# A decoder layer with a mixture of 64 experts: weight matrices in halves, a fifth ring slot, smaller gather chunks, quads spread out, and a shorter routing

## The chip, the cores and the metric

The kernel runs on one core of a Trainium2 chip. The core has TensorE (matrix products), VectorE, ScalarE and GpSimd, a sequencer SyncE that here only issues transfers, and 16 DMA engines that move data from the chip's memory (HBM) into the core's buffer (SBUF). Matrix products are written into PSUM, which has eight banks. The metric is the device time of one execution in microseconds (us); less is better.

## The reference

One decoder layer for 256 tokens of width 1024, in float32. A mixer (stick-breaking attention, a recurrent block, cross-attention to a memory) is added to the input; then comes a mixture of experts, which is where nearly all of the time goes:

```python
h = x + mixer(rms_norm(x))
t = rms_norm(h)                                    # 256 x 1024
scores = sigmoid(t @ w_router)                     # 256 x 64
choice = scores + router_bias
grp_score = top_k(choice.reshape(256, 8, 8), 2).sum(-1)
emask = expert's group is among the best 4 of 8 groups
eidx  = top_k(where(emask, choice, -inf), 8)       # 8 experts per token
w     = scores[eidx] / (sum + 1e-20) * 2.5
routed = sum over the experts e of
         gate[:, e] * ((silu(t @ w_gate[e]) * (t @ w_up[e])) @ w_down[e])
out = h + routed + shared_expert(t)
```

The gate and up matrices of an expert are 1024 x 256 each, its down matrix is 256 x 1024; each takes 1 MiB, so an expert takes 3 MiB and the 64 experts take 192 MiB, each of which is read once.

## The kernel before

The program is written by hand for each engine: an engine runs its own list of instructions in order and waits on semaphores, which other engines and the DMA queue raise. SyncE's list is the queue of all weight transfers, so a wait in it holds back everything that stands behind it.

**Up to the experts.** The mixer takes the first 145 us. Then the second norm (`second_norm`, for the token tiles t = 0 and 1 of 128 tokens), the router's product on TensorE, and `route(t)` on VectorE, which picks 8 experts for every token with small instructions that each wait for the one before. In the meantime TensorE runs the shared expert's gate and up products (`shared_gate_up`), and then the counts of tokens per expert (L1537 to L1547), which wait for `route(1)`. From the counts VectorE makes `pick`, a matrix of ones and zeros that says which token stands in which slot (`build_pick`), and an order of the experts by number of tokens (`permute`, `ids`). The normed tokens `xn2` are split into two parts, `xhi` (ScalarE, L736) and `xlo` (GpSimd, L549), so that a gather by products with `pick` keeps full precision.

**Groups.** The experts are worked off in 26 groups of 128 token slots: a pair is two experts with 64 slots each, a quad is four experts with 32 slots each, and the wide pair is two experts in two groups (the weights are used twice). The order is: two pairs of fixed experts (`FIXED = 4`; the weights can be loaded before the routing is known), two quads, the wide pair, 15 pairs, five quads. `group(g)` on TensorE is, in order:

1. `gate_up` (L1580): for k = 0..7 the products of the gathered rows with the gate and up matrices, into bank U; it first waits for `gu_loaded` of all of its experts, and at the end raises `gu_ps`.
2. a part of the gather of the next chunk (L1554). A chunk is four groups (the first one two groups), and its eight steps k are shared out among the groups of the chunk before; ScalarE (L755) and VectorE (L1244) copy each result into `xg`.
3. transposes of the hidden rows and of the slot matrix, 0.56 us (L1586 to L1594).
4. `scatter` of the group before (L1610).
5. `down` (L1602), which waits for `d_loaded` and raises `y_ps` at its end.

**The ring.** `RING = 4` slots of 24 KB per partition hold one expert each: `ring_gu` (16 KB) and `ring_d` (8 KB). SyncE's loop takes the groups in order. For each it waits for `gu_ps` of the group that used the slot, expert by expert, and issues the gate and the up matrix (L363, L364), then waits for `y_ps` and issues the down matrix (L367):

```python
for e, r in zip(g.experts, chosen):
    sp.wait_ge(gu_ps, gu_end[gu_taken[e]] + 1)
    load_gate_up(sp, e, ranked(w_gate_e, r, KD), ranked(w_up_e, r, KD))
for e, r in zip(g.experts, chosen):
    sp.wait_ge(y_ps, 2 * d_end[d_taken[e]] + 2)
    load_down(sp, e, ranked(w_down_e, r, KH))
```

Before the first group the experts 1, 2 and 3, the shared expert's matrices and the fourth down matrix are in place; the gate and up matrices of the fourth expert follow when the first group's `gate_up` has ended.

## Time and profile before

| what | value |
|---|---|
| median of 3 runs | 683.92 us (682.54 to 684.01) |
| the profiled execution | 686.89 us, its span from first to last instruction 685.0 us |
| mean granted TensorE clock | 0.934 of full speed |
| TensorE busy | 578.9 us (85%) |
| VectorE, ScalarE, GpSimd busy | 206.0, 142.0 and 24.2 us |
| moved | 225.89 MB, mean 330 GB/s over the span |

A row of the chain of waits tells when a piece of the work that ended last began and how long it took; a window tells how busy each engine was in a stretch, what clock TensorE was granted, and how many GB/s the transfers moved. L with a number is a line of the kernel. TensorE has two clock levels, 2.4 GHz (1.00) and 1.2 GHz (0.50).

### The profile page before, as it was taken

To read this page: it belongs to the slowest core of one execution; us is meant where nothing else is said; L and a number is where in the kernel's file an instruction comes from. 1 tells how busy PE (TensorE), PEld (TensorE's weight loads), DVE (VectorE), ACT (ScalarE), POOL (GpSimd) and SP (SyncE) were. 2 spreads that over 40 slices of the span, in tenths; PEclk is the share of its full clock that TensorE was granted. 3 is DMA by queue.
4 is the path that set the end of the run, shared out by engine and by line. 5 is a ranking of instruction groups with operands and counts; after the bars stand their busy time and mean duration, and the time that the engine had idled before them with its cause. 6 is when DMAs were issued, how large, how long until landed. Compare 5 with 4: busy or idle time off the path is not lost.

```text
span 685.0 us, 7647 instructions
## 1 busy us (share of the span) xinstructions
PE 578.9 (85%) x2905; PEld 298.0 (44%) x2906; DVE 206.0 (30%) x497; ACT 142.0 (21%) x268; POOL 24.2 (4%) x75
## 2 busy tenths in 40 slices
PE   8999998998998596999999999999996817263545
PEld 6887774455553242544444454444443302021212
DVE  2328476777225011222231123123111201010103
ACT  5434237352111010211111111121111101010101
POOL 1001113020000000000000000000000000000000
PEclk9999999999999988999999999999998959695869
DMA  8954349610679999599999999999989797999892
GB/s 259 376 172 184 135 173 329 272 62 1 250 287 402 425 370 423 216 403 397 409 417 423 419 418 416 420 421 420 421 372 379 312 425 318 422 377 422 343 424 74
DMA packets 40830, 225.89 MB, mean 330 GB/s; under 512 B 4064, under 2 KB 11272, under 8 KB 15832
## 3 DMA queue, kind: packets, MB, share of 16 engines
q1 hardware_dynamic: 39688, 223.38, 80.6%
q0 software_dynamic: 528, 1.87, 1.0%
q8 instruction: 24, 0.39, 0.2%
q10 hardware_dynamic: 576, 0.13, 0.1%
q14 instruction: 14, 0.11, 0.0%
HBM read 224.32 MB, written 1.05 MB: 329 GB/s over the span
## 4 chain that ended last, share of the span: by engine, by line
PE 71%; DMA 18%; SPq 3%; DVE 3%; issue 3%; ACT 2%; DVEq 0%; ACTq 0%
PE ps L1580 29%; DMA ring_gu<-in_w_up_e 17%; PE ps L1602 10%; PE ps L1554 7%; PE ps L1340 6%; PE ps L1610 5%; PE ps L1456 4%; PE ps L1357 3%; SPq L363 1%; SPq L364 1%; PE ps L1503 1%; PE ps L1347 1%; DMA x_in<-in_x 1%; PE ps L1586 1%; PE ps L1592 1%
## 5 line engine op out<-in xcount | busy, mean ns | idle before, releaser
L1580 PE MATMUL ps<-ring_gu,xg 128*64 128x512 f32 (+1 forms) x992 | 184.7, 657 | 85.5 <-DMA ring_gu<-in_w_up_e 77.3
L1580 PEld LDWEIGHTS ps<-ring_gu,xg 128*64 128x64 f32 (+1 forms) x992 | 57.4, 135 | 209.4 <-issue 209.4
L1602 PE MATMUL ps<-ring_d,e_hT 128*64 128x512 f32 (+1 forms) x528 | 94.9, 597 | 0.2 <-DVE xg L1244 0.2
L1211 DVE TENSOR_TENSOR e_h<-e_sg,ps 128x256 f32<-128x256 f32 x26 | 16.2, 622 | 249.6 <-ACT e_sg L759 249.6
L1277 DVE SCALAR_TENSOR_TENSOR ylo<-ps,gslot,yhi 128x512 fp32r<-128x512 f32 x52 | 39.0, 751 | 116.7 <-ACT yhi L774 116.7
L759 ACT ACTIVATE e_sg<-ps 128x256 f32<-128x256 f32 x26 | 10.0, 383 | 271.4 <-PE ps L1580 271.4
L774 ACT ACTIVATE yhi<-ps,gslot 128x512 fp32r<-128x512 f32 x52 | 35.7, 687 | 116.7 <-PE ps L1602 116.7
L1602 PEld LDWEIGHTS ps<-ring_d,e_hT 128*64 128x64 f32 (+1 forms) x528 | 26.9, 125 | 54.2 <-issue 54.1
L1610 PE MATMUL ps<-yhi,S 128*128 128x512 f32 x104 | 43.1, 415 | 1.6 <-ACT yhi L774 1.6
L1610 PE MATMUL ps<-ylo,S 128*128 128x512 f32 x104 | 40.9, 393 | 0.0
L1554 PE MATMUL ps<-pick,xhi 128*128 128x512 f32 (+1 forms) x112 | 37.7, 418 | 0.0
L1554 PE MATMUL ps<-pick,xlo 128*128 128x512 f32 (+1 forms) x112 | 33.6, 382 | 0.0
L1456 PE MATMUL ps<-wo,yT 128*128 128x512 f32 x64 | 29.3, 601 | 0.0
L1554 PEld LDWEIGHTS ps<-pick,xhi 128*128 128x128 f32 x112 | 19.3, 193 | 21.3 <-issue 18.6
L1340 PE MATMUL ps<-hT,wA 128*128 128x256 f32 x128 | 27.8, 379 | 0.0
L1340 PEld LDWEIGHTS ps<-hT,wA 128*128 128x128 f32 x128 | 24.2, 190 | 3.3
L1244 DVE COPY xg<-ps 128x512 f32<-128x512 f32 x24 | 16.6, 691 | 24.3 <-PE ps L1554 24.3
L1554 PEld LDWEIGHTS ps<-pick,xlo 128*128 128x128 f32 x112 | 20.9, 193 | 4.3
L1610 PEld LDWEIGHTS ps<-yhi,S 128*128 128x128 f32 x104 | 19.6, 189 | 6.0 <-ACT yhi L774 2.5
L1610 PEld LDWEIGHTS ps<-ylo,S 128*128 128x128 f32 x104 | 19.6, 189 | 3.5
L755 ACT COPY xg<-ps 128x512 f32<-128x512 f32 x24 | 14.1, 587 | 17.5 <-PE ps L1554 17.5
L1456 PEld LDWEIGHTS ps<-wo,yT 128*128 128x128 f32 x64 | 11.5, 190 | 12.6 <-issue 11.8
(334 smaller groups left out, 545.8 us busy)
## 6 DMA issues: line engine op xcount, KB each, us to landing
ring_gu<-in_w_gate_e SPq DMA_DIRECT2D x64, 1024.0 KB, 10.2
ring_gu<-in_w_up_e SPq DMA_DIRECT2D x64, 1024.0 KB, 12.3
ring_d<-in_w_down_e SPq DMA_DIRECT2D x64, 1024.0 KB, 12.4
wA<-in_w_in SPq DMA_DIRECT2D x4, 1024.0 KB, 9.5
wo<-in_w_out SPq DMA_DIRECT2D x1, 4096.0 KB, 13.1
wR<-in_w_in SPq DMA_DIRECT2D x3, 1024.0 KB, 16.4
wV<-in_w_in SPq DMA_DIRECT2D x1, 2048.0 KB, 15.5
w_kv<-in_w_mem_kv SPq DMA_DIRECT2D x1, 2048.0 KB, 18.9
```

What stands on the lines that cost most here:

```text
L755: nc.scalar.copy(xg[(g.chunk + 1) % 2][:, k, :], ps[:, Y[0], :]).then_inc(xg_act, 1)
L774: nc.scalar.mul(yhi[:, half * 512:(half + 1) * 512], ps[:, Y[half], :], gslot[:, g.index % 2:g.index % 2 + 1]).then_inc(yhi_act, 1)
L1211: nc.vector.tensor_tensor(dst[:].rearrange("q k p -> q p k"), e_sg[:].rearrange("q (p k) -> q p k", k=KH), ps[:, U, DE:2 * DE].rearrange(" ...
L1244: nc.vector.tensor_copy(xg[(g.chunk + 1) % 2][:, k, :], ps[:, Y[1], :]).then_inc(xg_dve, 1)
L1277: nc.vector.scalar_tensor_tensor(ylo[:, c], ps[:, Y[half], :], gslot[:, g.index % 2:g.index % 2 + 1], yhi[:, c].bitcast(F32), ALU.mult, AL ...
L1340: last = mm(b[:, 0:SEQ], w[:, k, c:c + P], hT[:, k, :], start=k == 0, stop=k == KD - 1)
L1357: last = mm(b, a[:, k, c:c + P], w[:, k, :], start=k == 0 and m == 0, stop=k == KD - 1 and m == 2)
L1456: last = mm(ps[:, ACC[2 * t + half], :], yT[:, k, t * P:(t + 1) * P], wo[:, k, half * 512:(half + 1) * 512], start=k == chunks[0], stop=k ...
L1554: last = mm(ps[:, Y[k % 2], 0:n], part[:, t, k, :], pick[c % 2][:, t, 0:n], start=i == 0, stop=i == 3)
L1580: last = mm(ps[side * w:(side + 1) * w, U, :], rows(k, slice(side * w, (side + 1) * w)), ring_gu[n][:, :, k, :], start=k == 0, stop=k == K ...
L1602: last = mm(ps[side * w:(side + 1) * w, Y[half], :], e_hT[:, kk, side * w:(side + 1) * w], ring_d[n][:, kk, half * 512:(half + 1) * 512], ...
L1610: last = mm(ps[:, ACC[2 * t + half], :], to_token[:, t * P:(t + 1) * P], y[:, half * 512:(half + 1) * 512], start=first and i == 0, stop=f ...
```

## The change

- Gate and up matrices are loaded in halves of four k each (two transfers of 0.5 MiB in place of one of 1 MiB, 4 KB per partition and transfer in place of 8 KB), with a semaphore for each half; `gate_up` waits for the first half of all experts of its group, then for the second, and raises `gu_ps` after each, so that a half of a slot is released alone. SyncE's loop issues all first halves of a group, then all second halves, then the down matrices.
- `RING = 5`: the fifth slot lies where `wo` and the first chunk's buffers were. Chunks are two groups (13 chunks; `xg` has 8 KB per buffer, `pick` 2 KB), a gather step does two k with 256 columns each, and `xlo` overwrites `xn2`. `s_d` is loaded in two pieces, late, and used in group 3.
- `FIXED = 6`: three pairs of fixed experts. The gate and up matrices and the down matrix of the fourth are issued as soon as the output projection is done; the fifth down matrix comes early too.
- The quads are spread: after the wide pair come three pairs and a quad, again and again (14 pairs, 5 quads); the last group is a quad, as before.
- Routing: two small `tensor_scalar` and one product less per tile, the memset once and ahead, `picked` written directly by the comparison; `repl` is made once for both tiles while TensorE counts. `xlo` is computed on VectorE, for tile 0 ahead of the second norm of tile 1, for tile 1 between the two calls of `route`; GpSimd has nothing left there. ScalarE makes `xhi` of tile 0 earlier.

```diff
-    FIXED, HALF, TABLE = 4, 32, 8
+    FIXED, HALF, TABLE = 6, 30, 8
+    STEPS, SHARED = KD // 2, 3
-    RING = 4
+    RING = 5
...
-    plan = [("pair", None)] * 2 + [("quad", quads.pop(0)), ("quad", quads.pop(0)), ("wide", 0)]
-    plan += [("pair", r) for r in pairs] + [("quad", r) for r in quads]
+    plan = [("pair", None)] * (FIXED // 2) + [("quad", quads.pop(0)), ("quad", quads.pop(0)), ("wide", 0)]
+    while pairs or quads:
+        plan += [("pair", pairs.pop(0)) for _ in range(min(3, len(pairs)))]
+        plan += [("quad", quads.pop(0))]
...
-    chunks = [groups[0:2]] + [groups[i:i + 4] for i in range(2, NG, 4)]
+    chunks = [groups[i:i + 2] for i in range(0, NG, 2)]
...
-            g.index, g.chunk, g.column, g.step = groups.index(g), c, i * P, i * (KD // len(members))
-            g.steps = KD // len(members) if c + 1 < len(chunks) else 0
+            g.index, g.chunk, g.column = groups.index(g), c, i * P
+            g.steps = range(2 * i, 2 * i + 2) if c + 1 < len(chunks) else range(0)
...
+    gu_at = [o_ring + 24 * KB * s for s in range(4)] + [o_A + 16 * KB]
+    d_at = [o_ring + 24 * KB * s + 16 * KB for s in range(4)] + [o_R + 8 * KB]
...
+        K_HALF = [slice(0, KD // 2), slice(KD // 2, KD)]
+
+        def load_gate_up(sp, e, h, gate_src, up_src):
             n = gu_slot[e]
-            sp.dma_start(ring_gu[n][:, 0], gate_src).then_inc(gu_loaded[n], 16)
-            sp.dma_start(ring_gu[n][:, 1], up_src).then_inc(gu_loaded[n], 16)
+            sp.dma_start(ring_gu[n][:, 0, K_HALF[h]], gate_src[:, K_HALF[h]]).then_inc(gu_loaded[n][h], 16)
+            sp.dma_start(ring_gu[n][:, 1, K_HALF[h]], up_src[:, K_HALF[h]]).then_inc(gu_loaded[n][h], 16)
...
             sp.wait_ge(wo_ps, len(projections))
-            sp.dma_start(s_d[:], w_down_sh[0].rearrange("(p k) n -> p k n", k=KH)).then_inc(s_d_loaded, 16)
-
-            sp.wait_ge(gu_ps, 1)
-            load_gate_up(sp, 4, expert(w_gate_e, 3, KD), expert(w_up_e, 3, KD))
+            for h in range(2):
+                fixed_gate_up(4, h)
+            sp.wait_ge(ssq_act, 6)
+            fixed_down(4)
+            shared_down_src = w_down_sh[0].rearrange("(p k) n -> p k n", k=KH)
+            sp.wait_ge(route_dve, 2)
+            sp.dma_start(s_d[0][:], shared_down_src[:, 0]).then_inc(s_d_loaded, 16)
+
+            for h in range(2):
+                for e in (5, 6):
+                    sp.wait_ge(gu_ps, 2 * gu_end[gu_taken[e]] + h + 1)
+                    fixed_gate_up(e, h)
+            sp.wait_ge(s_hT_ps, NT)
+            sp.dma_start(s_d[1][:], shared_down_src[:, 1]).then_inc(s_d_loaded, 16)
+            sp.wait_ge(y_ps, 2 * d_end[d_taken[6]] + 2)
+            fixed_down(6)
...
-                    for e, r in zip(g.experts, chosen):
-                        if gu_taken[e] == 0:
-                            sp.wait_ge(s_gu_ps, NT)
-                        else:
-                            sp.wait_ge(gu_ps, gu_end[gu_taken[e]] + 1)
-                        load_gate_up(sp, e, ranked(w_gate_e, r, KD), ranked(w_up_e, r, KD))
+                    for h in range(2):
+                        for e, r in zip(g.experts, chosen):
+                            if gu_taken[e] == 0:
+                                sp.wait_ge(s_gu_ps, NT)
+                            else:
+                                sp.wait_ge(gu_ps, 2 * gu_end[gu_taken[e]] + h + 1)
+                            load_gate_up(sp, e, h, ranked(w_gate_e, r, KD), ranked(w_up_e, r, KD))
...
-            for t in range(NT):
-                pool.wait_ge(split_act, t + 1)
-                pool.tensor_tensor(xlo[:, t], xn2[:, t], xhi[:, t].bitcast(F32), ALU.subtract).then_inc(split_pool, 1)
...
-                link(nc.vector.memset(grp[:, t, 12:16], -HUGE))
...
-                link(nc.vector.tensor_scalar(grp[:, t, 0:GROUPS], grep[:, t, 0:GROUPS], -1.0, 1.0, ALU.mult, ALU.add))
-                link(nc.vector.tensor_scalar(grep[:, t, 0:GROUPS], grep[:, t, 0:GROUPS], -HUGE, None, ALU.mult))
...
-                link(nc.vector.tensor_tensor(cg, choice[:, t, :].rearrange("p (g e) -> p g e", g=GROUPS), taken, ALU.mult))
-                link(nc.vector.tensor_tensor(cg, cg, off, ALU.add))
+                link(nc.vector.scalar_tensor_tensor(
+                    cand[:, t, :].rearrange("p (g e) -> p g e", g=GROUPS),
+                    grep[:, t, 0:GROUPS].unsqueeze(2).to_broadcast([P, GROUPS, EG]), -HUGE,
+                    choice[:, t, :].rearrange("p (g e) -> p g e", g=GROUPS), ALU.mult, ALU.add))
...
-                link(nc.vector.tensor_scalar(repl[:, t, :], repl[:, t, :], HUGE, None, ALU.is_equal))
-                nc.vector.tensor_copy(picked[:, t, :], repl[:, t, :]).then_inc(route_dve, 1)
+                nc.vector.tensor_scalar(picked[:, t, :], repl[:, t, :], HUGE, None, ALU.is_equal).then_inc(route_dve, 1)
...
+            low_part(0)
             second_norm(1)
...
             route(0)
+            low_part(1)
             route(1)
...
-            def gather_step(c, k):
-                n = P * len(chunks[c])
-                for i, (part, t) in enumerate(((xhi, 0), (xhi, 1), (xlo, 0), (xlo, 1))):
-                    last = mm(ps[:, Y[k % 2], 0:n], part[:, t, k, :], pick[c % 2][:, t, 0:n], start=i == 0, stop=i == 3)
+            def gather_step(c, step):
+                for k in (2 * step, 2 * step + 1):
+                    o = ps[:, Y[step % 2], k % 2 * 2 * P:(k % 2 + 1) * 2 * P]
+                    for i, (part, t) in enumerate(((xhi, 0), (xhi, 1), (xlo, 0), (xlo, 1))):
+                        last = mm(o, part[:, t, k, :], pick[c % 2][:, t, :], start=i == 0, stop=i == 3)
...
+                    if k % 4 == 0:
+                        for n, count in entries:
+                            pe.wait_ge(gu_loaded[n][k // 4], count)
...
+                    if k % 4 == 3:
+                        last.then_inc(sem, 1)
```

## Rows read from the trace of the kernel before

**Rows 1.** The page: the span, and GB/s in 40 slices of 17.1 us.

```profile
span 685.0 us, 7647 instructions
...
GB/s 259 376 172 184 135 173 329 272 62 1 250 287 402 425 370 423 216 403 397 409 417 423 419 418 416 420 421 420 421 372 379 312 425 318 422 377 422 343 424 74
```

**Rows 2.** Windows: us, busy us (xinstructions) of each engine, TensorE clock, DMA share, GB/s.

```profile
264.00:507.00 243.00, 243.00 (x1126) 111.09 (x1124) 58.94 (x122) 42.89 (x80) 0.00 (x0) 0.99 0.97 402
507.00:669.00 162.00, 89.45 (x582) 32.98 (x578) 17.35 (x42) 12.79 (x24) 0.00 (x0) 0.78 0.92 375
```

**Rows 3.** The chain of waits in order of time: start us, us, what.

```profile
280.77 6.87 PE ps L1580 x32
287.64 2.06 PE ps L1554 x8
290.26 1.96 PE ps L1610 x8
292.21 3.58 PE ps L1602 x16
...
541.87 20.00 DMA ring_gu<-in_w_up_e
562.23 9.89 PE ps L1580 x64
...
672.42 3.62 PE ps L1602 x32
```

**Rows 4.** Windows: four stretches of the transfers; the last begins at an issue.

```profile
24.00:38.00 14.00, 14.00 (x66) 12.32 (x66) 6.91 (x8) 7.49 (x10) 0.00 (x0) 1.00 1.06 374
82.00:90.00 8.00, 8.00 (x38) 5.94 (x38) 3.61 (x10) 1.62 (x4) 1.07 (x4) 1.00 1.02 414
113.00:129.00 16.00, 14.69 (x61) 7.37 (x60) 12.81 (x31) 5.79 (x15) 0.72 (x1) 1.00 1.01 423
176.72:186.72 10.00, 9.78 (x40) 6.24 (x42) 3.64 (x9) 2.68 (x6) 0.00 (x0) 1.00 0.88 360
```

**Rows 5.** The timeline, SyncE's queue: start us, us, engine line.

```profile
176.72 0.33 SPq L363 DMA_DIRECT2D ring_gu<-in_w_gate_e  x1
...
538.20 0.34 SPq L363 DMA_DIRECT2D ring_gu<-in_w_gate_e  x1
```

**Rows 6.** The chain of waits from 160 us to the first group of experts.

```profile
163.72 4.02 PE ps L1554 x24
...
168.51 1.15 PE ps L1554 x8
169.66 7.02 PE ps L1580 x32
176.68 4.49 PE ps L1503 x10
```

**Rows 7.** The timeline, TensorE: the counts of the routing, and what it waited for.

```profile
160.22 0.20 PE L1537 MATMUL ps<-picked,upper 128*128 128x64 bf16 x1 [2.82 <-DVE picked L1095]
```

**Rows 8.** The timeline, VectorE, the routing of both token tiles.

```profile
150.02 1.78 DVE L1079 TENSOR_TENSOR grp<-top 128x8 f32<-128x8 f32 x1
...
152.44 1.94 DVE L1084 TENSOR_TENSOR grep<-grep,grp 128x8 f32<-128x8 f32 x1
...
156.27 0.22 DVE L1073 TENSOR_TENSOR choice<-score,rbias 128x64 f32<-128x64 f32 x1
...
158.22 0.17 DVE L1085 TENSOR_SCALAR grp<-grep 128x8 f32<-128x8 f32 x1
...
158.89 0.23 DVE L1091 TENSOR_TENSOR cand<-cand,grep 128x64 f32<-128x64 f32 x1
...
159.96 0.20 DVE L1095 CAST picked<-repl 128x64 bf16<-128x64 f32 x1
```

**Rows 9.** The timeline, GpSimd, beside the routing.

```profile
149.41 2.37 POOL L549 TENSOR_TENSOR xlo<-xn,xhi 128x1024 fp32r<-128x1024 f32 x1 [17.15 <-ACT xhi L736]
```

**Rows 10.** Groups of instructions, VectorE, shapes kept apart.

```profile
L959 DVE TENSOR_TENSOR ca_sq<-ca_raw 128x1024 f32<-128x1024 f32 x1 | 1.2, 1212 | 0.0
```

More of the change, by code:

```diff
@@ L728, in _ @@
                     evac_x2T(0)
+                    nc.scalar.copy(xhi[:, 0], xn2[:, 0]).then_inc(split_act, 1)
             def scores(t):
@@ L1109, in _ @@
             dve.wait_ge(consts, 3)
+            link(nc.vector.memset(grp[:, :, 12:16], -HUGE))
             def shared_evac(t):
@@ L1115, in _ @@
             route(0)
+            low_part(1)
             route(1)
+            dve.wait_ge(route_dve, 2)
+            link(nc.vector.tensor_scalar(repl[:], repl[:], HUGE, None, ALU.is_equal))
             dve.wait_ge(count_ps, 1)
@@ L1517, in shared_down @@
                     last = mm(ps[:, ACC[2 * t + half], :], s_hT[:, kk, t * P:(t + 1) * P],
-                              s_d[:, kk, half * 512:(half + 1) * 512], start=False, stop=False,
+                              s_d[kk][:, half * 512:(half + 1) * 512], start=False, stop=False,
                               skip_group_check=True)
@@ L1524, in _ @@
             router(0)
-            pe.wait_ge(gu_loaded[0], 32)
+            for h in range(2):
+                pe.wait_ge(gu_loaded[0][h], 32)
             pe.wait_ge(x1_dve, 12)
@@ L1620, in extra_pair @@
                 for k in range(KD):
-                    for t in range(NT):
-                        last = mm(ps[:, Y[k // 4], k % 4 * P:(k % 4 + 1) * P], xn2[:, t, k, :],
-                                  ov_pick[:, t, :].bitcast(F32), start=t == 0, stop=t == NT - 1)
+                    for j, (part, t) in enumerate(((xhi, 0), (xhi, 1), (xlo, 0), (xlo, 1))):
+                        last = mm(ps[:, Y[k // 4], k % 4 * P:(k % 4 + 1) * P], part[:, t, k, :], ov_pick[:, t, :],
+                                  start=j == 0, stop=j == 3)
                     if k % 4 == 3:
@@ L1672, in group @@
                     pe.wait_ge(caps_dve, 1)
-                gate_up(lambda k, c: wide_rows[:, k, c0 + c.start:c0 + c.stop], [gu_slot[e] for e in g.experts], gu_ps,
+                gate_up(lambda k, c: source[:, k, c0 + c.start:c0 + c.stop], [(gu_slot[e], 32 * gu_fill[e]) for e in g.experts], gu_ps,
                         chunk=g.chunk if g is chunks[g.chunk][0] else None)
```

177 lines of the change are left out of this document (83 added, 94 removed).

## The prediction

> **What bounds the kernel now.** I read the page first, for GB/s: from the thirteenth slice on most slices stand at 415 to 425, with dips, and the ninth and tenth stand at 62 and 1 [rows 1]. A kernel that moves 192 MiB of expert weights is then to be read by its transfers. The windows cut that part into two regimes. While pairs run, TensorE is busy for all of 243.0 us and the transfers run at 402; while the last quads run, TensorE is busy for 89.45 of 162 us at a mean clock of 0.78 and the transfers run at 375 [rows 2]. The chain of waits says why. A group costs TensorE 6.87 (`gate_up`) + 2.06 (gather) + 0.56 (transposes, 289.70 to 290.26) + 1.96 (scatter) + 3.58 (down) = 15.03 us [rows 3], for a pair as for a quad. A pair brings 6 MiB = 6.29 MB, which at 424 GB/s takes 14.84 us: TensorE leads by a hair. A quad brings 12 MiB, 29.7 us, so there the transfers lead, TensorE waits (the last `up` matrix lands 20.00 us after its issue) and then runs `gate_up` at the lower clock, 1.2 GHz, in 9.89 us where a full-speed one takes 6.87 [rows 3]. During a quad's `gate_up` all four slots are in use and nothing can be issued before it ends (L363 at 538.20 [rows 5]), so each quad also costs idle transfers. The reader is to see two parts, each held by the resource that the other leaves free: in total TensorE needs 26 x 15.03 = 391 us, the transfers of the experts need about 475 us, and the kernel spends 685.0 - 169.66 = 515 us from the first group to the end [rows 1, 6]. Whatever lets the queue run without pauses from an earlier moment is worth its full length.
>
> What the queue does when it is full: 423 GB/s with the 8 KB runs of the expert matrices, 414 in the window that lies inside the `wo` transfer, whose runs are 4 KB, 374 in the window of the input projection's matrices, whose runs are 1 and 2 KB. From an issue at 176.72 the next 10 us bring 360 instead of 424, so the start costs 10 x (1 - 360/424) = 1.5 us [rows 4].
>
> **When the first group starts.** TensorE's shared work before the counts ends at 160.22 - 2.82 = 157.40; it then waits 2.82 us for `picked` [rows 7]. Routing of tile 1 takes 156.27 to 160.16. Of it the two `tensor_scalar` (0.20 each from start to start), one product of two (0.26), the memset (0.10) and the cast (0.20) go: about 1.0 of 3.9, so 2.9 are left [rows 8]. In tile 0 two instructions on eight elements take 1.78 and 1.94 us, beside 0.17 for one as small; both end when GpSimd's `xlo`, 2.37 us from 149.41 and its twin after it, ends [rows 8, 9]. With that work gone from GpSimd they shrink by 3.4 us. VectorE pays for `xlo` itself: 1.21 us each by a product of the same 128x1024 [rows 10]; the first lies in its wait for ScalarE's square ahead of the second norm (0 to 0.1 us on the path), the second is on it. So: 149.2 + 2.9 + 1.2 + 2.9 = 156.2, ahead of 157.4. The wait goes, and 1.2 us are to spare; without that cover each further us of routing would cost one. GpSimd's queue holds nothing behind the removed work, and ScalarE makes `xhi` of tile 0 (one copy of 1024 columns) while it waits for the residual of tile 1. The new `repl` over both tiles lies beside the counts.
>
> Then TensorE no longer pauses. Before, after the pause, the gather's 24 products took 4.02 us where the last 8 took 1.15 [rows 6], so 32 take 4.6 at full speed against 5.2; shared products in between were slow too (160.86 to 163.72 for four of the ten that take 4.49 [rows 6], so 1.8 instead of 2.9). I take 2.8 + 0.6 + 1.1 = 4.5 us: group 0 starts at 165.2 instead of 169.66. Bounds: 2.8 if the clock falls anyway, nothing if routing is late.
>
> **TensorE per group.** The gather has 16 products of 256 columns for 8 of 512. At 1.15/8 = 0.144 each [rows 6] that is 2.30 for 2.06, so 15.27 a group. Bounds: 2.06, and 16 x 0.19 (a 128x128 weight load, if that set the pace) = 3.0. The copies out of the banks keep their number and size. `build_pick` comes twice as often with half the work, while `gate_up` runs; the extra waits inside `gate_up` cost nothing when the halves are there. SyncE issues 16 halves for a quad in place of 8 matrices; at 0.33 us of an issue [rows 5], or 0.5 with what stands around it, that is 8 us beside 29.7 us of transfers, hidden while the queue is full.
>
> **Bytes and rate.** Before the first group ends its first half there are now expert 1 to 4 and down 5 in place; the transfers of expert 4, after the output projection, fall into the slices of 62 and 1 GB/s [rows 1], which is cover enough. Left are 60 x 2 MiB in halves, 59 down matrices and half of `s_d`: 179.5 MiB = 188.2 MB, 125.8 of them in runs of 4 KB. For those I take 418 GB/s, between 414 and 423 and nearer to the row with the same runs, whose stretch also has the ends of one transfer in it: 301.0 + 62.4/0.424 = 147.2, together 448.2 us, 420 GB/s, 2.50 us a MiB. Bounds: 444 and 451.
>
> At one place a rule of the Trainium skill speaks against the change. DMA: Bandwidth & Descriptors says to batch transfers to at least 1 MiB (section Bandwidth) and gives a fixed 2.0 us for each beside bytes/436e3 us (section Anatomy of one DMA); were it paid for each half one after the other, 240 x 3.2 + 60 x 4.4 = 1030 us would come out, an estimate from that page. The rows disagree for queued transfers: 1 MiB each runs at 423 GB/s, 2.5 us [rows 4], not 4.4.
>
> **Pauses of the queue.** Bytes start at 165.2 + 3.4 (half of 6.87) + 1.5 = 170.1; before, the issue came at 176.72 [rows 5]. I follow SyncE's list against TensorE's clock.
> - Experts 5 and 6, 4 MiB, to 180.1. Behind them stands the wait for the shared transposes: group 0 has 6.9 + 4.5 + 2.3 + 0.6 + 0.4, so 179.9, bytes at 181.4: pause 1.3. The half of `s_d` ends at 182.6; down 6 waits for the end of group 0, 183.7, bytes at 185.2: pause 2.6.
> - Down 6 and the first halves of experts 7, 8, 9, 4 MiB, to 195.2. Expert 10, the fourth of the quad, needs the slot of a fixed expert of group 2, and all behind it waits. Group 1 ends at 183.7 + 15.3 + 0.8 = 199.8; group 2's first half at 203.2, bytes at 204.7: pause 9.5.
> - From then on 48 MiB are free to go before the next such spot (expert 26, fourth of the first spread quad): to 324.6. TensorE: group 2 to 215.1; group 3 with the shared down (7.1) and 2.3 of waits to 239.7; group 4 waits 5.9 for its second halves and pays 2.7 for the clock, 263.5; two to 280.8; then 15.3 each, group 9 starts at 326.7, its first half ends at 330.1, bytes at 331.6: pause 7.0.
> - Then three pairs and a quad bring 30 MiB, 74.9 us, against 4 x 15.3 + 2.7 on TensorE: the slots come free before the queue gets to them, and there is no pause. 123 MiB x 2.50 = 307.1, to 638.7.
>
> Sum: 170.1 + 448.2 + 20.4 = 638.7. The last down matrices arrive while TensorE is past `gate_up`; `down` to the end took 685.0 - 672.42 = 12.6 us [rows 1, 3], and data is usable up to 2.8 us after my count of bytes (538.20 + 1.5 + 19.8 against 562.23 [rows 3, 5]; I take 1.8). 638.7 + 1.8 + 12.6 = 653.1 for the span, against 685.0. The profiled execution's span is 1.1 above the median of the runs, so 652.0. Followed in the same way, the kernel before pauses for 5.5 us near 193 and for 8.3 us near 281; its slices 12 and 17 lack 17.1 x (1 - 287/424) = 5.5 and 17.1 x (1 - 216/424) = 8.4 us [rows 1], which is my ground for trusting the pauses.
>
> **Rivals.**
> *Halves run slower.* This is the case on the other side: shorter runs and twice as many transfers. (It is the mechanism of the Trainium skill's page DMA: Bandwidth & Descriptors, section Bandwidth.) If 4 KB halves went at the 374 GB/s of the shortest runs [rows 4], 336.4 in place of 301.0 us: 652 + 35 = 687. It decides at 125.8/(301.0 + 31.9) = 378 GB/s. Against it: 414 with the same runs. 4%.
> *The queue in order starves at every quad.* Pauses of 7 us at the four later quads too, less what TensorE catches up: 652 + 14 = 666, at worst 680. For it: one blocked fourth expert holds all behind it. Against: 75 us of transfers for 64 us of products. 17%.
> *The queue hardly pauses.* No pause at 324.6 and 423 for all: 652 - 7 - 4 = 641. It needs TensorE earlier at group 9 by 7 us, for which I see little. 10%.
> *TensorE is dearer* (16 x 0.19 a group): 0.7 more in each of the eight groups up to the second large pause, 652 + 6 = 658, within my range; later it hides.
> *No effect:* only if the quads' waits come back elsewhere in full, 2%.
>
> **Numbers.** My own case, 646 to 660, 67%. With the case below and most of the starving one the range is 642 to 668. A difference under 0.2% is about what a measurement of this kernel can't tell from none: faster 0.93, same 0.02, slower 0.05.
>
> **What will show it.** Windows of 350 to 600 at 418 to 422 GB/s with no idle; group 0 at 165.2 and no wait of the counts for `picked`; the two slow instructions at 0.2 us; a pause near 195 to 205 and one near 325 to 332; TensorE's waits for gate and up spread over the quads in pieces of 2 to 6 us, not 15. I am wrong if the full queue stands under 410 in the halves, or if windows between 350 and 600 show idle transfers while SyncE waits for `gu_ps`.

## The result, and the profile after

The changed kernel takes 669.53 us in the median of four runs (668.13 to 670.6), beside 683.96 us (682.54 to 686.55) of the kernel before on the same chip: a ratio of 0.9775 with the interval 0.9753 to 0.9797. It is faster, as forecast, but by 14.4 us where 31.9 were forecast, and 1.5 us outside the range of 642 to 668. The miss in the median is 17.5 us (669.53 against 652.0). It has two parts. The span of the profiled execution is 667.3 us where the sum had 653.1, so 14.2 us are of the kernel. The other 3.3 us come from the last step, from span to median: the forecast took off 1.1, because the one profiled execution before had a span 1.1 above the median; after the change the profiled span lies 2.2 below the median. That is the scatter of single executions, not a matter of the kernel, and without it the median would lie inside the range.

The page of the changed kernel, to be laid beside [rows 1]; GB/s is in 40 slices of 16.7 us:

```profile
span 667.3 us, 8385 instructions
...
GB/s 256 375 196 189 80 236 274 342 68 155 283 253 278 418 411 411 413 412 414 267 328 414 409 413 411 417 411 412 412 408 415 414 412 412 394 413 413 411 398 93
DMA packets 59699, 225.95 MB, mean 339 GB/s; under 512 B 6160, under 2 KB 13368, under 8 KB 51464
```

Two things are to be seen. From the twenty-second slice on there is not one dip as deep as those that [rows 1] show to the end: the queue stays full. But the level is 408 to 417 in all of them but three (394, and 398 and 93 at the end), where [rows 1] has 416 to 425 wherever nothing stops it. And the slices 20 and 21 (317 to 350 us) stand at 267 and 328. The windows say it in figures (columns as in [rows 2]):

```profile
165.00:200.00 35.00, 34.96 (x176) 16.80 (x174) 9.92 (x29) 6.46 (x13) 0.00 (x0) 1.00 0.74 255
165.00:345.00 180.00, 166.58 (x914) 78.55 (x914) 45.44 (x125) 27.87 (x53) 0.00 (x0) 0.98 0.90 348
...
198.00:204.00 6.00, 6.00 (x30) 2.01 (x28) 4.48 (x16) 0.82 (x2) 0.00 (x0) 1.00 0.06 23
204.00:208.00 4.00, 2.88 (x18) 1.42 (x15) 3.08 (x16) 0.39 (x1) 0.00 (x0) 1.00 0.92 236
328.00:335.00 7.00, 7.00 (x36) 2.35 (x34) 1.50 (x2) 1.30 (x2) 0.00 (x0) 1.00 0.09 32
340.00:345.00 5.00, 5.00 (x25) 1.73 (x27) 0.75 (x1) 1.02 (x2) 0.00 (x0) 1.00 1.00 271
400.00:600.00 200.00, 169.37 (x934) 77.43 (x932) 39.40 (x93) 27.60 (x51) 0.00 (x0) 0.91 1.02 411
...
645.00:650.00 5.00, 5.00 (x32) 1.25 (x24) 0.00 (x0) 0.00 (x0) 0.00 (x0) 0.56 0.94 392
650.00:655.00 5.00, 3.77 (x30) 2.28 (x26) 1.64 (x6) 0.76 (x2) 0.00 (x0) 1.00 0.31 129
```

The chain of waits gives the times of the steps (it answers to [rows 3, 6]); the line numbers of `gate_up`, gather, scatter and `down` are now L1607, L1578, L1638 and L1630:

```profile
159.87 2.87 PE ps L1578 x24
...
164.65 7.02 PE ps L1607 x32
...
206.00 0.91 DVE pick L1154 x4
207.04 2.14 PE ps L1578 x16
...
275.42 2.11 PE ps L1578 x16
...
329.54 3.46 PE ps L1607 x16
...
628.43 15.96 DMA ring_gu<-in_w_up_e
...
644.53 6.09 PE ps L1607 x32
...
652.55 1.97 PE ps L1638 x8
654.52 3.67 PE ps L1630 x32
```

TensorE does not pause before the first group (the 24 gather products behind the counts take 2.87 us where [rows 6] have 4.02), and group 0 starts at 164.65. The two slow instructions of [rows 8] now stand at 0.17 us, in the timeline of VectorE:

```profile
150.26 0.17 DVE L1100 TENSOR_TENSOR grp<-top 128x8 f32<-128x8 f32 x1
...
150.95 0.17 DVE L1104 TENSOR_TENSOR grep<-grep,grp 128x8 f32<-128x8 f32 x1
```

SyncE's queue in the timeline, the last issue ahead of each of the two long waits and the first behind it:

```profile
189.19 0.56 SPq L367 DMA_DIRECT2D ring_gu<-in_w_up_e  x1
202.66 0.33 SPq L366 DMA_DIRECT2D ring_gu<-in_w_gate_e  x1
...
319.56 0.35 SPq L367 DMA_DIRECT2D ring_gu<-in_w_up_e  x1
333.49 0.34 SPq L366 DMA_DIRECT2D ring_gu<-in_w_gate_e  x1
```

And the waits of TensorE (total us, times, longest):

```profile
PE ps L1607 <- DMA ring_gu<-in_w_up_e: 57.1, 21, 6.3
```

**Where the 14.2 us went.** By the forecast 154.5 us of transfers at 420 GB/s, 64.9 MB, would have been moved by 345 us (from 170.1, less 20.4 of pauses). The window 165 to 345 has 180 x 348 = 62.6 MB. The 2.3 MB that are missing cost 5.5 us at 411 GB/s; of these 3.4 are the rate (154.5 x 420/411 = 157.9) and 2.1 are longer pauses and dips. After 345 us 123.3 MB were left in the forecast: 293.6 us at 420, 300.0 at 411, 6.4 more. By this count the last byte is due at 650.6, and the span ends 16.7 later instead of 14.4: 2.3 more. Two things meet there. The transfers thin out (129 GB/s from 650 to 655). And by the chain TensorE's own way is as long: the last `up` matrix lands at 644.39, the second half of the last `gate_up` takes, after 4.45 us without work, 6.09 us (granted clock 0.56 from 645 to 650) where a half at full speed takes 3.46 (329.54 above), and `down` starts at 654.52 right behind the scatter, with no wait for a transfer in between. Together 3.4 + 2.1 + 6.4 + 2.3 = 14.2. The rate alone is 9.8 of it.

That is an account of where the difference lies, not yet its cause. Two questions went to the chip: what halves do to the rate, and whether the two large pauses, which the forecast held for a given, were the ring's or the list's.

### The profile page after: what moved, and what is told of

It is laid out like the page before. It is cut to its first block, busy times and chain, and to the rows that moved or that the text cites. A ratio compares the mean times of both kernels' runs of the same rounds, so it can differ in the third digit from the quotient of the medians.

```text
span 667.3 us, 8385 instructions
## 1 busy us (share of the span) xinstructions
PE 590.5 (88%) x3097; PEld 311.1 (47%) x3098; DVE 204.8 (31%) x513; ACT 141.5 (21%) x264; POOL 20.5 (3%) x81
## 4 chain that ended last, share of the span: by engine, by line
PE 60%; DMA 25%; SPq 8%; ACT 3%; DVE 2%; issue 2%; DVEq 0%; ACTq 0%
DMA ring_gu<-in_w_up_e 24%; PE ps L1607 20%; PE ps L1630 8%; PE ps L1362 6%; PE ps L1578 5%; SPq L367 4%; PE ps L1638 4%; SPq L366 4%; PE ps L1478 4%; PE ps L1379 3%; PE ps L1525 2%; PE ps L1369 1%; DMA x_in<-in_x 1%; PE ps L1335 1%; PE ps L1440 1%
## 5 line engine op out<-in xcount | busy, mean ns | idle before, releaser
L1607 PE MATMUL ps<-ring_gu,xg 128*64 128x512 f32 (+1 forms) x1056 | 210.7, 693 | 57.1 <-DMA ring_gu<-in_w_up_e 57.1
L1607 PEld LDWEIGHTS ps<-ring_gu,xg 128*64 128x64 f32 (+1 forms) x1056 | 65.1, 140 | 198.8 <-issue 198.6
L1630 PE MATMUL ps<-ring_d,e_hT 128*64 128x512 f32 (+1 forms) x528 | 94.9, 597 | 3.0 <-issue 3.0
L1630 PEld LDWEIGHTS ps<-ring_d,e_hT 128*64 128x64 f32 (+1 forms) x528 | 27.4, 125 | 56.6 <-issue 56.6
L1578 PE MATMUL ps<-pick,xhi 128*128 128x256 f32 x208 | 45.0, 298 | 1.1 <-DVE pick L1154 1.1
L1638 PE MATMUL ps<-yhi,S 128*128 128x512 f32 x104 | 43.2, 415 | 1.6 <-ACT yhi L795 1.6
L1578 PEld LDWEIGHTS ps<-pick,xhi 128*128 128x128 f32 x208 | 32.1, 190 | 21.3 <-issue 21.2
L1578 PE MATMUL ps<-pick,xlo 128*128 128x256 f32 x208 | 41.8, 282 | 0.0
L1638 PE MATMUL ps<-ylo,S 128*128 128x512 f32 x104 | 40.9, 393 | 0.0
L1578 PEld LDWEIGHTS ps<-pick,xlo 128*128 128x128 f32 x208 | 32.2, 191 | 0.0
L1638 PEld LDWEIGHTS ps<-yhi,S 128*128 128x128 f32 x104 | 19.6, 189 | 5.9 <-ACT yhi L795 2.5
L1638 PEld LDWEIGHTS ps<-ylo,S 128*128 128x128 f32 x104 | 19.6, 189 | 3.5
## 6 DMA issues: line engine op xcount, KB each, us to landing
ring_d<-in_w_down_e SPq DMA_DIRECT2D x64, 1024.0 KB, 17.1
```

The source lines that it names most:

```text
L1578: last = mm(o, part[:, t, k, :], pick[c % 2][:, t, :], start=i == 0, stop=i == 3)
L1607: last = mm(ps[side * w:(side + 1) * w, U, :], rows(k, slice(side * w, (side + 1) * w)), ring_gu[n][:, :, k, :], start=k == 0, stop=k == K ...
L1630: last = mm(ps[side * w:(side + 1) * w, Y[half], :], e_hT[:, kk, side * w:(side + 1) * w], ring_d[n][:, kk, half * 512:(half + 1) * 512], ...
L1638: last = mm(ps[:, ACC[2 * t + half], :], to_token[:, t * P:(t + 1) * P], y[:, half * 512:(half + 1) * 512], start=first and i == 0, stop=f ...
```

## The experiments

Ratios are to the kernel before, with their intervals. "Whole" means that each gate and up matrix is one transfer of 1 MiB. All cuts of code are excerpts; "..." marks what is left out.

### The queue by itself

Five kernels only transfer the experts' matrices, through a ring of five slots, with no products; each was executed once. `s_whole_8k` has whole matrices in runs of 8 KB; `s_half_4k` the halves in the order of the change; `s_whole_4k` whole matrices cut into the same runs of 4 KB; `s_half_8k` halves by partitions; `s_first_halves` all first halves and then all second ones, without the down matrices.

```
# s_whole_8k
sp.dma_start(ring_gu[s][:, 0], rows(w_gate_e, e, KD))
# s_whole_4k
sp.dma_start(ring_gu[s][:, :, H[0]], rows(w_gate_e, e, KD).rearrange("p (h k) n -> p h k n", h=2))
# s_half_4k, s_first_halves
sp.dma_start(ring_gu[s][:, 0, H[h]], rows(w_gate_e, e, KD)[:, H[h]])
# s_half_8k, Q[h] = 64 partitions
sp.dma_start(ring_gu[s][Q[h], 0], rows(w_gate_e, e, KD)[Q[h]])
```

> Only the transfers of the 64 experts (192 MiB, 201.3 MB), in whole matrices of 1 MiB with 8 KB runs, one after the other through five slots; no products, the output is zeros. Both theories expect the 423 GB/s of the queue before the change: 476 us of transfers, 480 to 488 us in all.

> The same bytes, but gate and up in halves of 0.5 MiB with 4 KB runs, in the order of the changed kernel (pairs: first halves, second halves, downs); no products, zeros out. Theory H (the halves themselves fill the queue less well): 412 GB/s as in the changed kernel's windows of 400 to 500 us, so 488 us of transfers, 12 us more than the whole matrices. Rival K (the lower rate comes from what runs beside the transfers in the kernel): no difference, within 1 us of the whole matrices.

> Whole matrices of 1 MiB, but laid down so that each run is 4 KB; as many transfers as with 8 KB runs. If the run's length is the price (H1), it costs the same 12 us as the halves; if the number of transfers and their semaphore writes is the price (H2), it costs nothing.

> Halves of 0.5 MiB with 8 KB runs (64 partitions each), as many transfers as in the changed kernel. H1 (run length): as fast as whole matrices with 8 KB. H2 (number of transfers): 12 us slower, like the halves with 4 KB runs.

> Only transfers, no products, zeros out: the first halves of gate and up of all 64 experts, then all second halves, without down matrices (128 MiB, 134.2 MB). Theory D (a queue that holds only halves of one kind, each leaving out every other 4 KB of the memory, moves less, as after the pauses of the changed kernel, 217 to 303 GB/s): 240 to 300 GB/s throughout, 450 to 560 us. Rival (the low rate belongs to the first microseconds after an idle queue): 413 GB/s, 325 us and some 10 around it.

The spans are 486.2, 498.5, 495.6, 832.9 and 338.4 us. Of the 12.3 us between the first two, 9.4 come with the run length alone (`s_whole_4k`) and 2.9 between that and the halves, which differ from it in the number and in the order of the transfers. `s_half_8k` says nothing on the number: with half of the partitions in a transfer it took 1.7 times as long, which neither H1 nor H2 foresaw. Windows of three of them, in the middle and at the start (columns: us, VectorE, GpSimd, clock, DMA share, GB/s); first `s_whole_8k`:

```profile
20.00:300.00 280.00, 0.00 (x0) 0.00 (x0) 1.00 1.01 422
```

then `s_whole_4k`:

```profile
20.00:300.00 280.00, 0.00 (x0) 0.00 (x0) 1.00 1.02 414
...
3.00:4.00 1.00, 0.00 (x0) 0.00 (x0) 1.00 0.97 385
4.00:5.00 1.00, 0.00 (x0) 0.00 (x0) 1.00 1.05 426
```

and `s_half_4k`:

```profile
20.00:300.00 280.00, 0.00 (x0) 0.00 (x0) 1.00 1.02 413
...
3.00:4.00 1.00, 0.00 (x0) 0.00 (x0) 1.00 0.99 266
4.00:5.00 1.00, 0.00 (x0) 0.00 (x0) 1.00 0.87 201
5.00:6.00 1.00, 0.00 (x0) 0.00 (x0) 1.00 0.81 233
6.00:8.00 2.00, 0.00 (x0) 0.00 (x0) 1.00 1.02 412
```

The full queue makes no difference between 1 MiB and 0.5 MiB: 414 and 413. It is the run that counts, 4 KB or 8 KB. The low start of the halves is not the lot of first halves as such: `s_first_halves` has 262, 242, 205 and 225 GB/s from 2 to 6 us, and then 409 from 20 to 300, with nothing but first halves. That refutes theory D and bears out its rival. So in a stream of nothing but halves the gate and up matrices go at 409, where the forecast took 418. Two parts of 409 and one of 422 (the down matrices keep runs of 8 KB) give 413, which is what both mixed streams show.

### The parts of the change

`whole` is the changed kernel with whole matrices, released when `gate_up` has ended:

```diff
-            sp.dma_start(ring_gu[n][:, 0, K_HALF[h]], gate_src[:, K_HALF[h]]).then_inc(gu_loaded[n][h], 16)
-            sp.dma_start(ring_gu[n][:, 1, K_HALF[h]], up_src[:, K_HALF[h]]).then_inc(gu_loaded[n][h], 16)
+            sp.dma_start(ring_gu[n][:, 0], gate_src).then_inc(gu_loaded[n][0], 16)
+            sp.dma_start(ring_gu[n][:, 1], up_src).then_inc(gu_loaded[n][0], 16)
...
-                    for h in range(2):
+                    for h in (1,):
...
-                    if k % 4 == 0:
+                    if k == 0:
```

> The changed kernel with gate and up matrices loaded whole (1 MiB, 8 KB runs) and released when gate_up ends; all else as changed. Theory H (halves cost rate, 412 against 420 GB/s, and release in halves brings about 3 us by the prediction's own count of the queue): the full queue back at 420, about 9 us less for rate and 3 to 4 us more for pauses, so 662 to 665 us. Rival K (rate is not of the halves): 412 stays and the early release is missed, 672 to 676 us.

656.43 us, 0.9569 (0.9542 to 0.9596): 13 us faster than with halves. Loading in halves, which the forecast had as the part that shortens the pauses, is the part that takes half of the gain back. Theory H was right on the rate, but with 662 to 665 it took the release in halves for a small gain and left out the order of the halves, which is taken apart further down. Windows of `whole`:

```profile
165.00:345.00 180.00, 168.22 (x928) 79.77 (x930) 46.84 (x131) 28.43 (x54) 0.00 (x0) 0.97 0.90 364
...
400.00:600.00 200.00, 168.16 (x952) 78.65 (x949) 39.14 (x93) 27.56 (x51) 0.00 (x0) 0.92 1.01 421
```

421 beside 411 in the same stretch, and 364 beside 348 up to 345 us, although a whole matrix needs the end of `gate_up`, not its middle.

`spread_only` adds the spread quads to the kernel before; `unspread` and `whole_unspread` take them out of the changed kernel and of `whole`:

```diff
-    while pairs or quads:
-        plan += [("pair", pairs.pop(0)) for _ in range(min(3, len(pairs)))]
-        plan += [("quad", quads.pop(0))]
+    plan += [("pair", r) for r in pairs] + [("quad", r) for r in quads]
```

> The kernel before with the quads spread (three pairs, a quad) and nothing else. Theory: the quads' waits for transfers (some 15 us each for the last four) are paid for by the transfers that run ahead in the pairs; with four slots and whole release a quad still stops the queue once. Expected 665 to 672. Rival (four slots can't hold a quad and its successor, so each quad stalls as before): 680 to 686.

> The changed kernel with the quads at the end as before. Theory (spreading is the largest part): the pairs are set by TensorE at 15.1 us while the transfers have nothing to make up, and the quads at the end by the transfers; only the pauses between quads are shorter by the halves: 676 to 682. Rival (fifth slot and halves do most): 667 to 672.

> Whole matrices, five slots, six fixed experts, the quads at the end. If spreading pays only when the transfers can run at full rate (the count of the queue gives 2 us for it), 657 to 660; if spreading costs something, as the pair 669.5 (spread) and 667.2 (at the end) with halves suggests, 653 to 656.

1.001 (0.9991 to 1.0028), 0.9745 (0.9723 to 0.9767) and 0.9574 (0.9555 to 0.9592, beside 0.9569 of `whole`): the spreading is worth nothing, with four slots or with five. The expectations that gave it a price (665 to 672 for `spread_only`, 676 to 682 for `unspread`) missed. It is a balance of two effects. Without the spreading TensorE waits longer at the end and less in the middle, and the pause at the first late quad is not gone but comes later (337 and 331 GB/s in the slices 30 and 31 of `unspread`). So `whole_unspread` moves more up to 345 us (376 GB/s from 165 to 345 beside 364 of `whole`) and less after it (414 from 345 to 500 us and 415 from 500 to 625, beside 421). With halves it is the same: 369 beside 348, then 402 and 400 beside 412 and 411. Spreading together with the order of `adjacent_release`, below, was not taken apart.

`route_only` gives the kernel before the short routing and `xlo` on VectorE, with `x1_sq` moved to free room:

```diff
-            for t in range(NT):
-                pool.wait_ge(split_act, t + 1)
-                pool.tensor_tensor(xlo[:, t], xn2[:, t], xhi[:, t].bitcast(F32), ALU.subtract).then_inc(split_pool, 1)
...
+            low_part(0)
...
+            low_part(1)
```

> The kernel before with the shorter routing and xlo on VectorE only (the square's scratch moved by 4 KB so that it doesn't meet xlo). The first group starts 4.5 to 5 us earlier; the rest follows, so 679 to 680. Rival (the start is early, but the transfers set the rest and take it back): 683 to 684.

680.76 us, 0.9944 (0.9922 to 0.9966): 3.8 us less, near the 679 to 680 expected. Its group 0 starts at 165.18 us, 4.5 before the 169.66 of [rows 6].

`whole_ring4` is `whole` with four slots. `FIXED = 6` and the rest stay; the fixed experts that have no slot at the start, the fourth among them, follow as slots come free; beside the line shown, only these loads are put in another order:

```diff
-    RING = 5
+    RING = 4
```

> Whole matrices and all else of the changed kernel (six fixed experts, chunks of two groups, spread quads, short routing), but four slots; the fourth expert's gate and up wait again for the first group. The count of the queue gives 31 us more than with five slots: 680 to 688. Rival (the early start of the routing and the small chunks carry the gain, the slot only its own 3 MiB, 7.4 us): 662 to 666.

684.04 us, 0.9973 (0.9956 to 0.9989), as the theory had it. With all other parts in place the fifth slot, and the earlier loads that it allows, is worth 27.6 of the 29 us of `whole`. The parts do not add up: the routing alone brings 0.56% in `route_only`, and all parts but the slot together 0.27%. The slot alone, in the kernel before, was not run; its room comes from the smaller chunks. Windows of `whole_ring4`, late:

```profile
345.00:500.00 155.00, 133.41 (x742) 62.67 (x739) 31.36 (x73) 22.15 (x41) 0.00 (x0) 0.93 0.96 396
500.00:625.00 125.00, 97.25 (x544) 44.10 (x545) 22.65 (x55) 15.94 (x29) 0.00 (x0) 0.88 0.96 396
```

and of `whole`:

```profile
345.00:500.00 155.00, 131.73 (x752) 61.36 (x748) 32.16 (x75) 21.84 (x41) 0.00 (x0) 0.92 1.01 421
500.00:625.00 125.00, 106.43 (x597) 49.81 (x586) 25.45 (x60) 18.43 (x34) 0.00 (x0) 0.94 1.01 421
```

With four slots a quad holds all of them, and the queue dips once a quad: of the slices after 376 us in the page of `whole_ring4` three stand at 330 to 341 GB/s, 70 to 85 us apart as the quads are, and the others at 415 to 424 up to the last one. With five it does not, 396 against 421.

### What in the halves costs 13 us

`whole_4k` is `whole` with the runs of 4 KB; like `whole` it waits for the whole matrices before `gate_up`, while the versions in halves wait for half by half. `half_major` is the changed kernel, halves in its own order, but each half waits for the end of the whole `gate_up`. `half_adjacent` is `half_major` with both halves of an expert one behind the other. `adjacent_release` is the changed kernel with nothing else than that order.

```diff
# half_major
-                                sp.wait_ge(gu_ps, 2 * gu_end[gu_taken[e]] + h + 1)
+                                sp.wait_ge(gu_ps, 2 * gu_end[gu_taken[e]] + 2)
# adjacent_release, the only edit
-                    for h in range(2):
-                        for e, r in zip(g.experts, chosen):
+                    for e, r in zip(g.experts, chosen):
+                        for h in range(2):
```

> The version with whole matrices (656.4 us; transfers of 1 MiB, released at the end of gate_up), laid down so that every run is 4 KB: first half of gate, first half of up, second half of gate, second half of up. Theory: the run length is three quarters of the lower rate (9.4 of 12.3 us with transfers alone, of which some 300/475 fall into the full stretch that sets the end), so 662 to 664. Rival (the 13 us between halves and whole matrices are pauses and dips at restarts): 656 to 658.

> The changed kernel, halves in its own order (all first halves of a group, then all second halves), but a slot is released only when gate_up has ended. Theory O (the order is what costs: behind the blocked first half of a quad's fourth expert stand three second halves, 3 MiB, 7.5 us, that whole matrices have behind them already at the pause): still there, so 669 to 673. Rival N (the number of transfers and dips cost it): the same 669 to 673; this run is the base for the next.

> As half_major, but first and second half of each expert are issued one behind the other. Theory O: the 3 MiB go ahead of the pause, 7 to 9 us less than half_major, 661 to 664, near the whole matrices in 4 KB runs (660.9). Rival N (256 more transfers and their dips): no change against half_major.

> The changed kernel with only the order turned: first and second half of an expert one behind the other, each half released alone as in the change. Theory O: 660 to 663, and what release in halves is worth is its distance to half_adjacent (the count gives 1 to 3 us). Rival N: 669 to 670, as changed.

| kernel | order of the halves | released | us | ratio | GB/s 165:345 | 400:600 |
|---|---|---|---|---|---|---|
| `half_major` | by half | whole | 677.42 | 0.9893 (0.9868 to 0.9919) | 337 | 410 |
| the change | by half | by half | 669.53 | 0.9775 (0.9753 to 0.9797) | 348 | 411 |
| `whole_4k` | none, 4 KB runs | whole | 660.93 | 0.9642 (0.9627 to 0.9658) | 368 | 413 |
| `half_adjacent` | by expert | whole | 658.53 | 0.9629 (0.9602 to 0.9656) | 370 | 413 |
| `whole` | none, 8 KB runs | whole | 656.43 | 0.9569 (0.9542 to 0.9596) | 364 | 421 |
| `adjacent_release` | by expert | by half | 654.11 | 0.9554 (0.9527 to 0.9580) | 379 | 413 |

Each cause can be read between two rows. The order alone: 0.9775 to 0.9554, 15 us, and 0.9893 to 0.9629, 18 us. The runs: `whole` to `whole_4k`, 5 us. The number of transfers (128 more): `whole_4k` to `half_adjacent`, no difference clear of noise, and 413 GB/s in both late windows. This pair also differs in when `gate_up` may start, so it shows only that the two together are worth nothing. The release by halves: `half_adjacent` to `adjacent_release`, 5 us, and 8 us in the other order, more than the expectations gave it (1 to 3): so `half_major` is slower than the 669 to 673 expected, and `half_adjacent` (661 to 664) and `adjacent_release` (660 to 663) are faster. Theory O holds in its direction, rival N falls. SyncE's queue in `adjacent_release` shows how the order does it:

```profile
192.81 0.40 SPq L367 DMA_DIRECT2D ring_gu<-in_w_up_e  x1
202.56 0.33 SPq L366 DMA_DIRECT2D ring_gu<-in_w_gate_e  x1
...
318.95 0.43 SPq L367 DMA_DIRECT2D ring_gu<-in_w_up_e  x1
327.84 0.33 SPq L366 DMA_DIRECT2D ring_gu<-in_w_gate_e  x1
```

and its chain of waits has group 9 at:

```profile
324.23 6.87 PE ps L1607 x32
```

It waits from 193.2 for the same thing as the change from 189.8, the slot of the quad's fourth expert. But twelve transfers have gone out since 186.50 instead of six since 186.60: the second halves of experts 7, 8 and 9, whose room was free in both kernels, no longer stand behind the blocked first half of expert 10. Those are 3 MiB, 7.6 us of transfers, during which the queue is not idle. At the next quad it is the same, and there the pause goes: by then TensorE has waited less for matrices and starts group 9 at 324.23 instead of 329.54, so the queue's wait ends at 327.84 instead of 333.49. Windows of `adjacent_release`:

```profile
165.00:200.00 35.00, 34.95 (x176) 16.76 (x174) 9.93 (x28) 6.36 (x13) 0.00 (x0) 1.00 0.82 291
165.00:345.00 180.00, 171.31 (x966) 80.12 (x966) 46.78 (x127) 28.12 (x53) 0.00 (x0) 0.98 0.98 379
320.00:345.00 25.00, 25.00 (x153) 10.46 (x155) 5.56 (x11) 4.09 (x7) 0.00 (x0) 1.00 1.02 406
```

406 GB/s from 320 to 345 us, where the change has its pause. By 345 us 68.2 MB are moved, 5.6 more than in the change; at 413 GB/s that is 13.6 us, of the 14.8 by which the span is shorter (652.5). What is left lies in the rate, 413 for 411.

The Trainium skill says in DMA: Bandwidth & Descriptors, section Bandwidth, to batch transfers to at least 1 MiB. Its measurements there, and those behind the fixed 2.0 us that the forecast cites, are of transfers issued from GpSimd; here SyncE issues them. For queued transfers of this kernel the runs do not bear that out: `half_adjacent`, with 256 transfers of 0.5 MiB, takes what `whole_4k` takes with 128 of 1 MiB in the same runs (0.9629 and 0.9642).

### Smaller suspects

`whole_last` loads only the last quad in halves, so that TensorE may start its last `gate_up` earlier. `hoist` reads the numbers of the next group's experts ahead of the waits (SyncE spends 3.05 us on four such reads before 186.60, while expert 7 could go). `pick_first` is `whole_last` with `list_extra`, 24 small instructions on VectorE, each behind the one before, moved behind the picks of the second chunk.

```diff
# pick_first
+                if g.index == 2:
+                    dve.wait_ge(caps_dve, 1)
+                    list_extra()
...
-                if g.index == 1:
-                    dve.wait_ge(caps_dve, 1)
-                    list_extra()
# hoist
+            chosen = choose(order[0])
...
+                    if at + 1 < len(order):
+                        chosen = choose(order[at + 1])
```

> The changed kernel with whole matrices (the version of 656.4 us), but the last quad's gate and up in halves. In the trace of the whole version the last quad's gate_up starts when all of its 8 MiB have landed and ends after the last down matrix; in the changed kernel the second half alone is left. Theory: 4 to 5 us shorter than whole, 651 to 653. Rival (the last down matrices set the end either way): 655 to 657.

> The changed kernel with SyncE's reads of the next group's expert numbers placed before its waits (3 us between the issues at 183.2 and 186.6 are such reads). Theory V (they delay the transfers and all that follows): 3 us less than the changed kernel, 666 to 667. Rival (the following pause is ended by TensorE's group 2, not by the queue, so nothing moves): 669 to 670.

> Whole matrices with the last quad in halves (654.4 us), and list_extra, 5.4 us of small VectorE work, behind the picks for group 3 in place of ahead of them. It takes away 1.1 us for which group 2's gather waited for its picks. If TensorE's way to the pause at 330 us sets the end, 653 to 654; if it is taken up by the quads' waits for transfers, no change, 654 to 655.

`whole_last` is at 0.9568 (0.9545 to 0.9592), no difference to `whole`, where 4 to 5 us were expected. `hoist` is at 0.9778 (0.976 to 0.9795), none to the change: the first issue comes at 184.03 instead of 186.60, but the wait still ends at 202.56. `pick_first` is at 0.9524 (0.9505 to 0.9542), 653.26 us, the lowest median: 3 us better by the ratio than `whole_last`, 1.2 us by the medians (654.44). In the changed kernel the gather of group 2 waits for its picks, because VectorE works through the list first:

```profile
200.49 0.21 DVE L1204 TENSOR_TENSOR cnt<-cnt,caps 128x64 f32<-128x64 f32 x1
...
205.82 0.15 DVE L1229 CAST n_extra<-end 128x1 int32<-128x1 f32 x1
206.00 0.90 DVE L1154 TENSOR_TENSOR pick<-iota,posv 128x128 fp32r<-128x128 f32 x4
```

In `pick_first` they change places, and the gather follows `gate_up` (200.76 + 6.87 = 207.63) with no wait:

```profile
202.20 0.89 DVE L1165 TENSOR_TENSOR pick<-iota,posv 128x128 fp32r<-128x128 f32 x4
203.00 0.22 DVE L1215 TENSOR_TENSOR cnt<-cnt,caps 128x64 f32<-128x64 f32 x1
```

That the wait is gone is shown; that it is what makes `pick_first` faster is not. The wait is 1.1 us long, and in the profiled executions TensorE reaches group 9 at 329.12 in `pick_first` and at 328.04 in `whole_last`, later and not earlier. The order of `adjacent_release` together with the picks of `pick_first` was not tried; it would show whether the two gains add up.

## Why the prediction was right and where it was wrong

**When the first group starts: right.** 165.2 was forecast, 164.65 came, with no wait for `picked`. The four shared products ahead of the gather take 1.91 us (1.8 in the forecast); the gather's 32 take 2.87 + 1.14 = 4.0 where 4.6 stood, which is most of the 0.5 us.

**TensorE per group: right in kind, 0.2 us too high.** The 16 gather products take 2.11 us, not 2.30.

**Bytes and rate: the step that failed, a mis-sized term.** For the 125.8 MB of halves I took 418 GB/s, between 414 and 423, although the row with the same runs had 414 [rows 4]. A stream of halves alone runs at 409, the mix with down matrices at 413, the changed kernel at 411. So 188.2 MB take 458 us instead of 448.2, and my upper bound of 451 did not hold them either, for the lower value that I allowed, 414, lies above the 409 that such a stream reaches. The term is 9.8 us short; with it put right and nothing else the forecast would have been 662, and 7.7 us off instead of 17.5. Of the 9.8 us some 7.5 are the length of the runs (188.2 MB at 413 GB/s take 455.7). The other 2.3 are 411 against 413: the kernels with the order by half stand at 410 and 411, those with the order by expert at 413; why is open.

**Pauses of the queue: right in place, in size together with the dips, wrong in cause.** Two pauses near 195 to 205 and 325 to 332 were forecast; issues resume at 202.66 and 333.49. The first, 9.5 us in the forecast, is some 6 us of idle queue (198 to 204 at 23 GB/s), for the transfers ahead of it ran slower than counted, and a dip follows it (236 GB/s from 204 to 208). The bytes moved by 200 us come out even: 35 x 255 = 8.9 MB, and 8.5 MiB in the forecast. The second, 7.0 in the forecast, is 6.5 us long by its window (328 to 335 at 32 GB/s), but some 3 us late, because group 9 starts at 329.54 rather than 326.7; 1.1 of that is the wait for the picks, which the forecast had at nothing. (The working's "two to 280.8" reads as two groups; its times only come out with one group of 15.3 and 2 us of waits, and group 6 starts at 283.62.) Of the 2.1 us that were missing by 345, most is the dip behind it, which I had not foreseen: 5 x (1 - 271/411) = 1.7. What was wrong is that I read both pauses as given by the ring and TensorE's pace. Turning two loops, with the same ring and the same instructions on TensorE, removes the second and feeds the first with 3 MiB more: 15 us. I had written that expert 10 blocks "all behind it" and did not ask what stood behind it, which is three second halves with their room free.

**What the parts bring: not priced in the forecast, and mostly misjudged in what was expected of the runs.** The spreading brings nothing and the halves take 13 us; with four slots the rest brings 0.3%. Without the fifth slot nearly all of the gain is gone. The forecast's opening reading of the quads, that all slots are in use during a quad's `gate_up` [rows 5], was the right one, and it points at a slot, not at halves.

**The end: 2.3 us more than forecast.** The forecast let the last down matrices set the end, with TensorE past `gate_up`. In the trace both ways are equally long: the transfers thin out over the last 5 us, and the second half of the last `gate_up` runs at the lower clock, 6.09 us for 3.46. Which of the two the 2.3 us belong to was not tested.

**The rivals.** *Halves run slower* is the true mechanism at a far smaller price: 409 for the halves, not 374. *The queue in order starves at every quad* put pauses at the four later quads as well, and there are none (411 GB/s from 400 to 600); that one blocked fourth expert holds back all behind it is nevertheless what costs 15 us, at the first two places. That 666 comes near 669.53 is luck. *The queue hardly pauses* has the missing second pause of `adjacent_release`, not its rate, and not the change. *TensorE is dearer* (2.11 us for the gather, not 3.0) and *no effect* fell.

Of the signs that I had named, no wait for `picked`, the two short instructions, the two pauses and TensorE's waits in pieces (57.1 us in 21, the longest 6.3) came true. The windows of 350 to 600 at 418 to 422 did not; with 411 they stand just over the 410 below which I would have called the theory wrong, and the stream of nothing but halves, at 409, stands under it.

## What to carry to other kernels

In a queue that runs in order, ask of each wait not only when it ends but what stands behind it with its room already free; put the transfers of one buffer side by side, so that a blocked one holds back as little as possible. Before cutting a load into pieces, compare what the early release brings (here 5 us) with what the shorter runs cost (here 5 us), and take the row with the same run length as the value of a price, with room on both sides of it, not as the end of a range. When several parts are changed at once, take out one at a time: here the one that relieves the stopped resource (the slot) takes nearly all of the gain with it, and a second remedy for the same stop (the spreading) none.

## What the runs showed of the hardware

- The rate of a full queue of expert matrices follows the run length: 422 GB/s with runs of 8 KB, 414 with whole matrices cut into 4 KB, 409 with nothing but halves of 4 KB. The size of a transfer (0.5 or 1 MiB) does not show in the full queue: 413 and 414.
- Where an idle queue is filled with such halves, the first 4 us run low: 201 to 274 GB/s in `s_half_4k`, 205 to 262 in `s_first_halves`, 236 in the changed kernel from 204 to 208 us, which is 1.6 to 1.7 us lost each time; with whole matrices in the same 4 KB runs the second microsecond is at 385 and the third at 426. After its second pause the changed kernel dips later, from 340 to 345 us, at 271 GB/s while its DMA engines are busy at a share of 1.00. The cause stays open; that it is a property of first halves as such was tried and fell.
- Transfers that cover only 64 of the 128 partitions are far slower: 832.9 us for what takes 486.2, when all gate and up matrices are loaded that way. An estimate from these two: with the 67.1 MB of down matrices taken off at 422 GB/s (159 us), 134.2 MB in 674 us are left, 199 GB/s, less than half of 422.
